# A decoder trunk: each layer opens with its input's norm, and two projections run through it by thirds

## The chip, the cores and the metric

One NeuronCore of one Trainium2 chip. The metric is the device time of one execution in microseconds. The kernel before took 3741.0 us, the median of three executions (3737.36 to 3747.48).

## The reference

Two layers over 1056 tokens of width 1024: a prompt of 1024 tokens, and eight samples of 4 tokens each with a cache of 2048 past tokens. All in float32. What matters here:

```python
h = layer_norm(x, ln0_g, ln0_b)
for l in range(2):
    u = h @ w_in[l]                      # 23 column tiles of 128: z, xbc, dt, q, k, v, qi, ki, wi, glu
    mix = concat(ssd(...), sparse_attention(...), conformer_conv(...)) @ w_out[l]
    h = layer_norm(ALPHA * h + mix, ln1_g[l], ln1_b[l])
    f = gated_causal_conv_ffn(h)         # w_up, width-3 convolution, silu gate, w_down
    h = layer_norm(ALPHA * h + f, ln2_g[l], ln2_b[l])
# returned: h, and the new keys, values, index keys, states and convolution histories of both layers
```

The sparse attention first scores all keys with small index vectors (qi, ki, wi); the samples' index keys lie in pages of 128 tokens in memory, which a page table names.

## The kernel before, in words

Activations lie with the 1024 channels on the partitions, as 8 tiles (KT) of 128 x 1056. A loop of the device (Fori, two rounds) holds one layer. The five engines' programs are written by hand and meet in semaphores. A layer has six stages; each ends in a barrier in which every engine drains and waits for the other three (Stages.end, L459 to 462; the lines L461 and L466 of the trace are its waits and those of the loop's barrier). At the loop's head a second barrier (between_layers, L464) lets SyncE clear all semaphores of a layer.

The norms ln0 (of the input, ahead of the loop), ln1 and ln2 work on three column groups of 352 tokens, the thirds. For ln0 and ln2, TensorE takes the mean of a third's total with one matmul against a matrix of 1/1024 (ln_mean, L781). VectorE subtracts it from the 8 tiles (L1667), ScalarE squares them into four buffers in turn (L1329), and TensorE adds the squares up, one matmul for each tile (ln_var, L797), which also frees the buffers. ScalarE takes the root (L1334), VectorE the reciprocal (L1672) and eight multiplies (L1677), ScalarE applies gain and bias and writes the result to X (L1344). A float32 matmul shows as two records in the trace. ln_all sets the order: VectorE subtracts in all three thirds and then does reciprocal and multiplies third by third; ScalarE squares all three thirds, and then does root and outputs third by third. ln0 works in place on X, ln2 on MIX. ln2 stands at the end of the loop's body, and the stage's barrier behind it.

At the start SyncE loads the input by thirds, then gains, constants and page table. In the loop it asks for the layer's vector VEC, the two convolution histories SSDH and CCH (these lie in tiles 6 and 7 of MIX), and then for a list of loads (LOADS) into a ring of 4 slots: three w_in tiles, six of the eight groups of index pages ("kidx", 16 pages to a group; each page is a register load and a DMA issue of its own, L422 and L423), then the other w_in tiles, and so on. A slot is loaded again when its user is done: the group in slot 0 waits for the product of the first w_in tile, the next two for those of the second and third. Groups 1 and 2 go to a buffer of their own; ScalarE issues them, 16 pages before the first product's copy and 16 between the second's and the third's (load_index_pages, called in ScalarE's loop over N_IDX).

The first stage's jobs (JOBS) are, in order: the first w_in tile (T_KI: index key, dt, wi), the second (T_QI), dup and rotdup (two small products with T_KI's copy), turn (its transposes), the third w_in tile, and two rotations. Jobs take two sets of three PSUM banks in turn; a set is free when ScalarE or VectorE has read it. After T_KI's copy, ScalarE and VectorE pass a softplus to and fro (L1757 to L1769, L1421, L1423); turn waits for its end. The second stage scores the index keys and turns the pages (L890).

When a layer is done, SyncE stores the first two thirds of X to yT, in both layers; the last third goes out behind the loop.

```python
            for t in range(THIRDS):
                ln_mean("ln0", t)
            for t in range(THIRDS):
                ln_var("ln0", t)
            pe.wait_ge(const_loaded, 48)
            with pe.Fori(0, DEPTH) as layer:
                between_layers(pe)
```

Of the kernel before, what the change touches and what calls it, by code (L numbers as in the profile page):

```python
# [182 lines left out]
def build(nc, xT, w_in, w_out, w_up, w_down, vec, ln0, const, pages, cache_k, cache_v, cache_kidx,  # L183
          ssm_in, ssd_in, cc_in, ffn_in, yT, kT_out, v_out, ki_out, ssm_p, ssm_s, ssd_out, cc_out, ffn_out):
    ctx = ExitStack()
    with ctx:
# [178 lines left out]
        def cache_page(name):  # L365
# [21 lines left out]
                                              "scaled", "out")}  # L387
        idx_full, idx_relu, idx_added = sem("index_products"), sem("index_relu"), sem("index_added")
# [133 lines left out]
        def ln_src(name, k, t):  # L522
            return third_of((MIX if name == "ln2" else X)[:, k, :], t)

        def ln_total(name, t):
            return {"ln0": third_of(WORK[:, 0:TOK], t), "ln1": TOTAL[:, t, :], "ln2": third_of(GATE[:, 0:TOK], t)}[name]
# [12 lines left out]
        def _(sp):  # L539

            for t in range(THIRDS):
                sp.dma_start(third_of(X[:, :, :], t), third_of(xT, t)).then_inc(x_loaded[t], 16)
# [4 lines left out]
            with sp.Fori(0, DEPTH) as layer:  # L547
# [78 lines left out]
        def _(pool):  # L626
# [8 lines left out]
            with pool.Fori(0, DEPTH) as layer:  # L635
# [91 lines left out]
                stage.end()  # L727
# [3 lines left out]
        def _(pe):  # L731
# [43 lines left out]
            def ln_mean(name, t):  # L775

                q = LN_FIRST[name] + t
                pe.wait_ge(tot["sum"], q + 1)
                if name == "ln1" and t:
                    pe.wait_ge(tot["centred"], KT * q)  # L780
                pe.matmul(mean_bank(name, t), MEAN[D_MODEL][:, :], ln_total(name, t), start=True, stop=True  # L781
                          ).then_inc(tot["mean"], 1)
# [9 lines left out]
            def ln_var(name, t):  # L792

                q = LN_FIRST[name] + t
                for k in range(KT):
                    pe.wait_ge(tot["squared"], KT * q + k + 1)
                    pe.matmul(var_bank(name, t), MEAN[D_MODEL][:, :], FOUR_SQUARES[:, k % 4, :], start=k == 0, stop=k == KT - 1  # L797
                              ).then_inc(tot["taken"] if k < KT - 1 else tot["var"], 1)
# [23 lines left out]
            for t in range(THIRDS):  # L822
                ln_mean("ln0", t)
# [1668 lines left out]
```

## Time and profile before

| | before |
|---|---|
| median of three executions | 3741.0 us |
| the profiled execution's own time | 3736.99 us |
| its span | 3735.2 us |
| busy share of TensorE, VectorE, ScalarE, GpSimd | 89%, 51%, 33%, 18% |
| chain of waits, share by engine | TensorE 66%, VectorE 15%, ScalarE 7%, SyncE's queue 6%, issue 3%, DMA 2% |
| granted TensorE clock, mean | 0.925 of full speed |

The span is the time from the first to the last instruction on the chip. Busy shares are means over the whole of it. The chain of waits is followed back from the last instruction, at each step to what released it; "issue" in it is time in which the engine waited for nothing that the profile shows. In the list of waits and in timelines, "idle" stands in square brackets, with what ended it behind an arrow. PE is TensorE, DVE VectorE, ACT ScalarE, POOL GpSimd, SP SyncE; a q behind it (SPq, ACTq) is that engine's instruction queue, where DMAs are issued.

### The profile page before, as it was taken

What the parts mean: (1) busy time and instruction counts of PE and PEld (TensorE: products, weight loads), DVE (VectorE), ACT (ScalarE), POOL (GpSimd) and SP (SyncE); (2) the same over time, 40 slices, a digit from 0 to 9 for tenths busy, and PEclk for the clock granted to TensorE, in tenths of its full rate; (3) what the DMA queues carried; (4) which work ended last, traced back from release to release, by engine and by line L of the source; (5) the groups of instructions that cost most, each with busy time, mean ns of one, the idle gap of its engine ahead of it and who ended that gap; (6) DMA issues with size and microseconds to landing.
All of it is one profiled execution on the core that took longest, in us unless ns stands there. A gap on an engine that the chain in (4) does not pass through costs nothing.

```text
span 3735.2 us, 51972 instructions
## 1 busy us (share of the span) xinstructions
PE 3315.5 (89%) x19418; PEld 2675.2 (72%) x19418; DVE 1898.2 (51%) x3006; ACT 1220.3 (33%) x2261; POOL 661.6 (18%) x661
## 2 busy tenths in 40 slices
PE   4899987877989999999868999887779999999995
PEld 2445465644889999999834544665459899999994
DVE  4569774331665434434435797633236644334335
ACT  3246713333342212212222656142343312212213
POOL 0000000011024333333100000000110333333321
PEclk8999998857999999999979999996689999999998
DMA  3111004305201111111021110242150111111111
GB/s 102 41 41 34 29 26 125 94 28 148 72 23 39 47 51 35 51 52 35 28 81 44 34 34 23 70 117 70 57 168 7 37 49 36 53 49 35 54 36 58
DMA packets 169896, 206.62 MB, mean 55 GB/s; under 512 B 61025, under 2 KB 138146, under 8 KB 168738
## 3 DMA queue, kind: packets, MB, share of 16 engines
q1 hardware_dynamic: 143138, 185.36, 16.5%
q10 hardware_dynamic: 26496, 17.84, 1.7%
q8 instruction: 156, 2.56, 0.3%
q14 instruction: 106, 0.87, 0.1%
HBM read 187.17 MB, written 15.96 MB: 54 GB/s over the span
## 4 chain that ended last, share of the span: by engine, by line
PE 66%; DVE 15%; ACT 7%; SPq 6%; issue 3%; DMA 2%; POOL 0%; ACTq 0%; DVEq 0%; POOLq 0%
PE PS L758 42%; PE PS L739 8%; DVE MIX L1708 4%; DVE WORK L1708 2%; SPq L432 2%; SPq L433 2%; PE PS L771 2%; ACT X L1344 2%; PE PS L843 2%; DVE WORK L1896 2%; PE PS L951 1%; ACT WORK L1469 1%; DMA RING<-cache_k 1%; PE PS L797 1%; DVE WORK L1672 1%
## 5 line engine op out<-in xcount | busy, mean ns | idle before, releaser
L758 PE MATMUL PS<-WORK_parts,WHIGH_parts 128*128 128x352 f32 x4224 | 869.5, 328 | 35.2 <-POOL WORK_parts L725 17.7
L758 PEld LDWEIGHTS PS<-WORK_parts,WHIGH_parts 128*128 128x128 f32 x4224 | 723.7, 191 | 38.9 <-issue 20.6
L739 PE MATMUL PS<-X,RING 128*128 128x512 f32 (+1 forms) x2016 | 670.5, 495 | 86.2 <-DMA RING<-w_in 65.8
L758 PE MATMUL PS<-WORK_parts,RING_parts 128*128 128x352 f32 x3168 | 690.8, 326 | 0.0
L739 PEld LDWEIGHTS PS<-X,RING 128*128 128x128 f32 x2016 | 337.9, 194 | 420.1 <-issue 351.0
L758 PEld LDWEIGHTS PS<-WORK_parts,RING_parts 128*128 128x128 f32 x3168 | 545.2, 190 | 0.0
L1708 DVE SCALAR_TENSOR_TENSOR WORK<-WORK,VEC 128x1072 f32<-128x1072 f32 (+1 forms) x236 | 477.3, 2022 | 8.4
L1293 ACT ACTIVATE WORK<-PS 128x32 f32<-128x32 f32 (+11 forms) x412 | 191.0, 514 | 825.1 <-PE PS L758 580.4
L497 POOL TENSOR_TENSOR RING_parts<-RING,WHIGH_parts 128x1024 fp32r<-128x1024 f32 (+2 forms) x184 | 372.1, 2022 | 461.4 <-ACT WHIGH_parts L1293 461.1
L758 PE MATMUL PS<-X_parts,WHIGH_parts 128*128 128x352 f32 x2016 | 435.0, 324 | 0.0
L758 PEld LDWEIGHTS PS<-X_parts,WHIGH_parts 128*128 128x128 f32 x2016 | 345.1, 189 | 0.0
L1706 DVE TENSOR_SCALAR WORK<-WORK,VEC 128x1072 f32<-128x1072 f32 (+1 forms) x90 | 70.6, 784 | 530.1 <-ACT WORK L1293 530.1
L1469 ACT ACTIVATE WORK<-WORK 128x512 bf16<-128x512 f32 x310 | 285.7, 923 | 164.1 <-DVE WORK L1943 164.0
L1293 ACT ACTIVATE WHIGH_parts<-RING 128x1024 fp32r<-128x1024 f32 (+2 forms) x188 | 155.5, 827 | 436.3 <-PE PS L758 418.0
L2316 DVE TENSOR_TENSOR MIX<-MIX,PS 128x1056 f32<-128x1056 f32 x80 | 100.3, 1254 | 286.5 <-PE PS L758 286.5
L771 PE MATMUL PS<-WORK_parts 128*128 128x352 f32 x576 | 144.6, 331 | 0.0
L1708 DVE SCALAR_TENSOR_TENSOR MIX<-WORK,VEC,MIX 128x1296 f32<-128x1296 f32 (+1 forms) x96 | 142.5, 1484 | 3.4
L725 POOL TENSOR_TENSOR WORK_parts<-WORK,WORK_parts 128x1056 fp32r<-128x1056 f32 x44 | 108.2, 2460 | 168.3 <-ACT WORK_parts L1293 168.3
L1293 ACT ACTIVATE WORK_parts<-WORK 128x1056 fp32r<-128x1056 f32 (+1 forms) x56 | 59.4, 1078 | 218.7 <-DVE WORK L2304 218.7
L951 PE MATMUL PS<-CONST,RING 128*128 128x128 f32 x512 | 82.4, 304 | 48.2 <-DMA RING<-cache_k 29.1
L2108 DVE CUSTOM_DVE_ANT_0 WORK<-PS,WORK 128x384 f32<-128x384 f32 (+5 forms) x48 | 41.7, 887 | 152.0 <-PE PS L1101 152.0
L1896 DVE TENSOR_SCALAR_CACHE_REDUCE WORK<-WORK 128x544 bf16<-128x544 f32 (+6 forms) x164 | 116.0, 743 | 0.3
(323 smaller groups left out, 3738.3 us busy)
## 6 DMA issues: line engine op xcount, KB each, us to landing
RING<-w_up SPq DMA_DIRECT2D x88, 512.0 KB, 3.6
RING<-cache_k SPq DMA_DIRECT2D x200, 128.0 KB, 2.2
RING<-cache_v SPq DMA_DIRECT2D x192, 128.0 KB, 2.1
RING<-w_in SPq DMA_DIRECT2D x46, 512.0 KB, 3.7
RING<-w_down SPq DMA_DIRECT2D x80, 256.0 KB, 2.7
RING<-cache_v ACTq DMA_DIRECT2D x64, 128.0 KB, 2.4
RING<-cache_k ACTq DMA_DIRECT2D x56, 128.0 KB, 2.6
yT<-X SPq DMA_DIRECT2D x5, 1408.0 KB, 5.5
```

Source lines behind the costliest of these rows:

```text
L432: page = eng.value_load(PT[0:1, at_page:at_page + 1], min_val=0, max_val=cache_k.shape[0] - 1)
L497: eng.tensor_tensor(low, raw, WHIGH[:, m % 2, 0:w].bitcast(F32), ALU.subtract).then_inc(done, 1)
L725: pool.tensor_tensor(HIDL[:, b, :], HID[:, b, :], HIDH[:, b, :].bitcast(F32), ALU.subtract).then_inc(hid_low, 1)
L739: mm = pe.matmul(job_psum(n, w, first=first), stationary(k), moving(k)[:, first:first + w], start=k == 0, stop=k == k_tiles - 1)
L758: mm = pe.matmul(thirds(n)[:, third, :], a, x[:, third * THIRD:(third + 1) * THIRD], start=k == 0 and part == 0, stop=k == tiles - 1 and p ...
L771: mm = pe.matmul(dst, a[:, w], third_of(x, t), start=k == 0 and part == 0, stop=k == KT - 1 and part == 2)
L951: mm = pe.transpose(key_bank(k)[:, (j % 2 * 2 + t) * P:(j % 2 * 2 + t + 1) * P], cache_page(name)[:, j, t * P:(t + 1) * P], c("ident"))
L1293: return act.activation(dst, src, ACT.Copy)
L1469: ins = act.activation(SCAN_ASIDE[s][:, 0:w], SEL[:, SEL_AT[i]:SEL_AT[i] + w], ACT.Sign, bias=SCAN_TRIED[:, s:s + 1], scale=SCAN_SCALE, ac ...
L1708: ins = dve.scalar_tensor_tensor(out=acc, in0=src[:, k:k + w], scalar=v(col + k), in1=acc, op0=ALU.mult, op1=ALU.add)
L1896: marks.append(step.mark(dve.tensor_scalar(ASIDE[len(marks) % 2][:, 0:x.shape[-1]], x, limit, None, op, ALU.add, accum_out=to)))
L2316: dve.tensor_tensor(y, y, thirds(n), ALU.add).then_inc(free[n % 2], 1)
```

## The change

ln0's place in the loop is the head of its body: in both rounds it norms what lies in MIX, which is the input in the first round and the first layer's sum in the second. ln2 stands behind the loop, once. Gains and biases come from LN0; in the fifth stage GpSimd copies ln2's into it. The sixth barrier of a layer is gone. The new norm has semaphores of its own (opening).

ln_all has a new order: VectorE subtracts in third t+1 before the reciprocal and the multiplies of third t; ScalarE squares third t+1 between the root and the outputs of third t. TensorE takes three means, two variances, then the first two w_in tiles' products of third 0 (open_third), the variance of third 2, and the products of thirds 1 and 2. SyncE asks for the three w_in tiles first; VEC comes ahead of page group 0; then SyncE issues page group 1 as well and waits for the norm's last output before it loads the histories. ScalarE issues 8 pages of group 2 behind the norm and 8 at the job dup. yT is stored once, by thirds, behind the loop.

```diff
 def ln_src(name, k, t):
-    return third_of((MIX if name == "ln2" else X)[:, k, :], t)
+    return third_of((X if name == "ln1" else MIX)[:, k, :], t)
...
 # SyncE
-    sp.dma_start(third_of(X[:, :, :], t), third_of(xT, t)).then_inc(x_loaded[t], 16)
+    sp.dma_start(third_of(MIX[:, :, :], t), third_of(xT, t)).then_inc(x_loaded[t], 16)
...
-    sp.dma_start(VEC[:, :], vec[layer, :, :]).then_inc(vec_loaded, 16)
-    sp.dma_start(SSDH[:, :, :], ssd_in[layer, :, :, :]).then_inc(hist_loaded, 16)
-    sp.dma_start(CCH[:, :, :], cc_in[layer, :, :, :]).then_inc(hist_loaded, 16)
     for n, name in enumerate(LOADS):
         kind, slot = name[0], n % NSLOT
+        if name == ("kidx", 0):
+            sp.dma_start(VEC[:, :], vec[layer, :, :]).then_inc(vec_loaded, 16)
+        elif n == NSLOT:
+            load_index_pages(sp, layer, KEPT_APART[0], 0, 16)
+            sp.wait_ge(opening["out"], KT * THIRDS)
+            sp.dma_start(SSDH[:, :, :], ssd_in[layer, :, :, :]).then_inc(hist_loaded, 16)
+            sp.dma_start(CCH[:, :, :], cc_in[layer, :, :, :]).then_inc(hist_loaded, 16)
...
-    for t in range(THIRDS - 1):
-        sp.wait_ge(tot["out"], KT * (LN_FIRST["ln2"] + t + 1))
-        store(third_of(yT, t), third_of(X[:, :, :], t))
-    sp.wait_ge(stored, 16 * 12)
-    sp.wait_ge(stage_done, 4 * 6)
-store(third_of(yT, THIRDS - 1), third_of(X[:, :, :], THIRDS - 1))
+    sp.wait_ge(stored, 16 * 10)
+for t in range(THIRDS):
+    sp.wait_ge(tot["out"], KT * (LN_FIRST["ln2"] + t + 1))
+    store(third_of(yT, t), third_of(X[:, :, :], t))
...
 # GpSimd, fifth stage
+    pool.tensor_copy(LN0[:, :], VEC[:, V_LN2G:V_LN2G + 2 * KT])
...
 # TensorE: the means and variances of ln0 ahead of the loop are gone; in the loop
-    for n in range(N_IDX):
+    def open_third(t):
+        for n in range(2):
+            w = weights(JOBS[n])
+            for k in range(KT):
+                pe.wait_ge(opening["out"], KT * t + k + 1)
+                mm = pe.matmul(thirds(n)[:, t, :], w[:, k, :], third_of(X[:, k, :], t),
+                               start=k == 0, stop=k == KT - 1)
+            if t == THIRDS - 1:
+                mm.then_inc(full[n % 2], 1)
+
+    for t in range(THIRDS):
+        ln_mean("ln0", t)
+    ln_var("ln0", 0)
+    ln_var("ln0", 1)
+    open_third(0)
+    ln_var("ln0", 2)
+    open_third(1)
+    open_third(2)
+    for n in range(2, N_IDX):
         project(n)
     stage.end()
...
 # ScalarE
 def ln_all(name, gcol, bcol, params):
-    for t in range(THIRDS):
-        ln_squares(name, t, range(KT))
+    ln_squares(name, 0, range(KT))
     for t in range(THIRDS):
         ln_rstd(name, t)
+        if t + 1 < THIRDS:
+            ln_squares(name, t + 1, range(KT))
         ln_out_parts(name, t, range(KT), gcol, bcol, params)
...
-ln_all("ln0", 0, KT, LN0)
 with act.Fori(0, DEPTH) as layer:
     between_layers(act)
+    ln_all("ln0", 0, KT, LN0)
+    load_index_pages(act, layer, KEPT_APART[1], 0, 8)
     act.wait_ge(vec_loaded, 16)
     act.activation(EXPA[:, :], VEC[:, V_ALOG:V_ALOG + SSD_HEADS], ACT.Exp)
...
     for n in range(N_IDX):
-        if n in (0, 2):
-            load_index_pages(act, layer, KEPT_APART[n // 2], 0, 16)
+        if n == 2:
+            load_index_pages(act, layer, KEPT_APART[1], 8, 8)
         project(n)
...
-    ln_all("ln2", V_LN2G, V_LN2B, VEC)
-    stage.end()
+ln_all("ln2", V_LN2G, V_LN2B, VEC)
...
 # VectorE
 def ln_all(name):
+    for k in range(KT):
+        ln_centre(name, 0, k)
     for t in range(THIRDS):
-        for k in range(KT):
-            ln_centre(name, t, k)
-    for t in range(THIRDS):
+        if t + 1 < THIRDS:
+            for k in range(KT):
+                ln_centre(name, t + 1, k)
         ln_inverse(name, t)
         for k in range(KT):
             ln_scale(name, t, k)
```

## Rows read from the trace of the kernel before

**Rows 1.** Chain of waits, start and boundary of the layers: start, length in us, what.

```profile
8.57 10.55 DMA PT<-pages
...
1857.75 12.07 PE PS L797 x40
...
1896.36 4.21 issue
...
1903.54 3.96 DMA RING<-w_in
```

**Rows 2.** Timeline, first projections of layer 0: start, us, engine, line, operation, [idle before].

```profile
66.10 17.43 ACTq L423 DMA_DIRECT2D WHIGH<-cache_kidx  x16
...
68.39 33.60 PE L739 MATMUL PS<-X,RING 128*128 128x512 f32 x96 [30.44 <-DMA RING<-w_in]
...
86.50 1.05 ACT L1293 ACTIVATE WORK<-PS 128x1056 f32<-128x1056 f32 x1 [21.19 <-PE PS L739]
...
92.86 1.08 ACT L1423 ACTIVATE MIX<-MIX 8x1056 f32<-8x1056 f32 x1 [0.75 <-DVE MIX L1763]
...
95.26 1.25 DVE L1769 TENSOR_TENSOR WORK<-WORK,MIX 8x1056 f32<-8x1056 f32 x1
...
101.91 5.97 PE L739 MATMUL PS<-WORK,CONST 64*128 64x512 f32 x12
...
109.79 16.08 PE L739 MATMUL PS<-X,RING 128*128 128x512 f32 x48
```

**Rows 3.** Timeline, the norm ahead of layer 0 and the first barrier.

```profile
19.15 10.44 DVE L1667 TENSOR_TENSOR X<-X,PS 128x352 f32<-128x352 f32 x24
...
38.07 2.35 DVE L1672 RECIPROCAL WORK<-WORK 128x352 f32<-128x352 f32 x1 [8.49 <-ACT WORK L1334]
...
41.02 4.68 ACT L1344 ACTIVATE X<-X,LN 128x352 f32<-128x352 f32 x8 [2.98 <-DVE X L1677]
...
62.46 1.28 ACT L1376 ACT_TABLE_LOAD   x1 [0.56 <-SPq L553]
```

**Rows 4.** Timeline, end of layer 0 and start of layer 1.

```profile
1855.13 1.40 DVE L2325 TENSOR_TENSOR WORK<-WORK,MIX 128x352 f32<-128x352 f32 x3
...
1857.16 13.24 ACT L1329 ACTIVATE WORK<-MIX 128x352 f32<-128x352 f32 x24 [8.87 <-DVE MIX L1667]
...
1948.94 16.39 PE L739 MATMUL PS<-X,RING 128*128 128x512 f32 x48
```

**Rows 5.** Timeline of SyncE's queue in layer 0: the page loads.

```profile
66.89 77.98 SPq L423 DMA_DIRECT2D RING<-cache_kidx  x64
...
146.51 37.41 SPq L423 DMA_DIRECT2D RING<-cache_kidx  x32
```

**Rows 6.** SyncE's waits, 60 to 250 us: us in total, times, longest.

```profile
SPq L422 <- PE PS L739: 3.2, 2, 1.9
```

**Rows 7.** Timeline of TensorE, end of the index stage in layer 1.

```profile
2025.28 0.44 PE L890 MATMUL PS<-CONST,RING 128*128 128x128 f32 x2 [1.52 <-DMA RING<-cache_kidx]
```

**Rows 8.** Windows: us, then busy us of each engine (instructions), granted clock, DMA.

```profile
25.00:36.00 11.00, 11.00 (x37) 6.95 (x37) 4.59 (x11) 8.76 (x18) 0.00 (x0) 1.00 0.00 1
68.00:73.00 5.00, 4.61 (x6) 2.02 (x7) 0.00 (x0) 0.00 (x0) 0.00 (x0) 0.50 0.77 244
1975.00:1985.00 10.00, 9.91 (x28) 4.30 (x28) 6.43 (x23) 2.92 (x4) 1.48 (x1) 0.52 0.13 28
```

**Rows 9.** ScalarE's groups by line: roots and their table loads (busy us, mean ns).

```profile
L1334 ACT ACTIVATE WORK<-PS,EPSC 128x352 f32<-128x352 f32 x15 | 8.2, 546 | 7.9 <-PE PS L789 7.8
...
L1334 ACT ACT_TABLE_LOAD x5 | 6.4, 1283 | 0.1
```

**Rows 10.** Timeline, the last norm and the stores of y.

```profile
3689.46 10.44 DVE L1667 TENSOR_TENSOR MIX<-MIX,PS 128x352 f32<-128x352 f32 x24
...
3712.80 17.02 SPq L560 DMA_DIRECT2D yT<-X  x3
...
3724.29 4.68 ACT L1344 ACTIVATE X<-MIX,VEC 128x352 f32<-128x352 f32 x8 [2.98 <-DVE MIX L1677]
```

More of the change, by code:

```diff
@@ L387, in build @@
                                               "scaled", "out")}
+        opening = {n: sem("opening_" + n) for n in ("mean", "centred", "squared", "taken", "var", "rstd", "inverse",
+                                                    "scaled", "out")}
         idx_full, idx_relu, idx_added = sem("index_products"), sem("index_relu"), sem("index_added")
@@ L522, in ln_src, with ln_sems @@
         def ln_src(name, k, t):
-            return third_of((MIX if name == "ln2" else X)[:, k, :], t)
+            return third_of((X if name == "ln1" else MIX)[:, k, :], t)
+        def ln_sems(name):
+            return opening if name == "ln0" else tot
         def ln_total(name, t):
-            return {"ln0": third_of(WORK[:, 0:TOK], t), "ln1": TOTAL[:, t, :], "ln2": third_of(GATE[:, 0:TOK], t)}[name]
+            return TOTAL[:, t, :] if name == "ln1" else third_of(GATE[:, 0:TOK], t)
         def mean_bank(name, t):
@@ L1281, in _ @@
                                       lambda k: pe.wait_ge(hid_low, first + k + 1))
-                for t in range(THIRDS):
-                    ln_mean("ln2", t)
-                for t in range(THIRDS):
-                    ln_var("ln2", t)
-                stage.end()
+            for t in range(THIRDS):
+                ln_mean("ln2", t)
+            for t in range(THIRDS):
+                ln_var("ln2", t)
         @block.scalar
@@ L1344, in ln_out_parts @@
                     act.activation(third_of(X[:, k, :], t), src, ACT.Identity, bias=bias, scale=scale
-                                   ).then_inc(tot["out"], 1)
+                                   ).then_inc(sems["out"], 1)
             def ln_all(name, gcol, bcol, params):
-                for t in range(THIRDS):
-                    ln_squares(name, t, range(KT))
+                ln_squares(name, 0, range(KT))
                 for t in range(THIRDS):
                     ln_rstd(name, t)
+                    if t + 1 < THIRDS:
+                        ln_squares(name, t + 1, range(KT))
                     ln_out_parts(name, t, range(KT), gcol, bcol, params)
@@ L1415, in project @@
                                else KTL[:, j - T_K, :] if j < T_Q else QT[:, j - T_Q, :])
-                        copy(dst, job_psum(n)).then_inc(f, 1)
+                        if n < 2:
+                            copy(in_thirds(dst), thirds(n)).then_inc(f, 1)
+                        else:
+                            copy(dst, job_psum(n)).then_inc(f, 1)
                     if j == T_KI:
@@ L1662, in ln_centre @@
             def ln_centre(name, t, k):
[L1663 removed]
+                q, sems = LN_FIRST[name] + t, ln_sems(name)
                 if k == 0:
[L1665 removed]
+                    dve.wait_ge(sems["mean"], q + 1)
                 s = ln_src(name, k, t)
[L1667 removed]
+                dve.tensor_tensor(s, s, mean_bank(name, t), ALU.subtract).then_inc(sems["centred"], 1)
             def ln_inverse(name, t):
[L1670 to L1673 removed]
+                q, sems = LN_FIRST[name] + t, ln_sems(name)
+                dve.wait_ge(sems["rstd"], q + 1)
+                dve.reciprocal(RSTD[:, t, :], RSTD[:, t, :]).then_inc(sems["inverse"], 1)
+                dve.wait_ge(sems["inverse"], q + 1)
             def ln_scale(name, t, k):
                 s = ln_src(name, k, t)
[L1677 removed]
+                dve.tensor_tensor(s, s, RSTD[:, t, :], ALU.mult).then_inc(ln_sems(name)["scaled"], 1)
             def ln_all(name):
+                for k in range(KT):
+                    ln_centre(name, 0, k)
                 for t in range(THIRDS):
[L1682 to L1684 removed]
+                    if t + 1 < THIRDS:
+                        for k in range(KT):
+                            ln_centre(name, t + 1, k)
                     ln_inverse(name, t)
@@ L2325, in _ @@
                                     dve.tensor_tensor(total, total, ln_src("ln2", j, t), ALU.add).then_inc(tot["sum"], 1)
-                ln_all("ln2")
-                stage.end()
+            ln_all("ln2")
 def _constants():
```

45 lines of the change are left out of this document (17 added, 28 removed).

## The prediction

> **What bounds the kernel now.** I read the page's busy shares first: TensorE is busy 89% of the span and heads the chain of waits, so what the change can win lies in stretches where TensorE stands still. Next the chain, at the three places where a norm stands alone: the start, the boundary between the layers and the end. At the start the chain runs through the load of the page table, which lands at 8.57 + 10.55 = 19.12 us, then through the norm, then through the first weights (the boundary shows 3.96 us of waiting for w_in) [rows 1]; the timeline shows TensorE's first projection at 68.39 us, after 30.44 us idle [rows 2]. At the boundary there is also a stretch of 4.21 us in which nothing runs, directly after the stage's end and before the loop's first instruction [rows 1]: the return to the loop's head.
>
> Last I followed the norm and the first projections in the timelines. In the norm every engine works in blocks of three thirds: all 24 subtractions (10.44 us), all squares (13.24 us at the boundary), then, third by third, a reciprocal of 2.35 us and eight multiplies, with eight outputs behind them [rows 3, 4]. TensorE has little to do in it, and afterwards two projections in a row (33.60 us for two) while ScalarE and VectorE wait [rows 2]. Behind that, SyncE's queue is nearly the bound up to the end of the index stage: it issues 32 page loads in 37.41 us (18.7 us for a group of 16), waits for TensorE only 3.2 us in the first 190 us of the layer, and TensorE waits 1.52 us for its last pages [rows 5 to 7]. Whatever moves the third w_in projection's end moves the rest with it, since the next SyncE group is issued at just that point and every stage ends in a barrier. I call this end T, counted from the release of the loop's barrier, B.
>
> **Before, per layer.** Layer 0: B would lie at 19.12 + 0.56 = 19.7 us (0.56 us is what the barrier took [rows 3]); the third projection ends at 109.79 + 16.08 = 125.9 [rows 2], that is T = 106.2. Layer 1: the totals of ln2 are ready at 1855.13 + 1.40 = 1856.5 [rows 4]. With the changed order the loop's return comes first: 4.2 + 0.1 + 0.6 us of barrier give B = 1861.4. The third projection ends at 1948.94 + 16.39 = 1965.3 [rows 4], T = 103.9.
>
> **After, step by step, in us after B.** A 352-column matmul takes 12.07/40 x 2 = 0.60 us at the full clock [rows 1], 1.2 at half. TensorE comes out of an idle stretch, so its granted clock is taken as half for 5 us, as at 68 to 73 us [rows 8].
> - Three means 3.6; variance of third 0: one matmul at half, seven at full: 9.0. VectorE subtracts third 0 from 1.2 and third 1 behind it, out of the way.
> - ScalarE squares until 8.4, loads the table of the root (1.28, as now) and takes it (0.55 [rows 9]): 10.2. Squares of third 1 (13.24/24 = 0.55 each [rows 4], behind matmuls of 0.60): 15.0. The reciprocal (2.35) ends at 12.6 beside it. Outputs of third 0 (4.68 [rows 3]): 19.7.
> - TensorE follows the outputs: first projection of this third 20.3, second 25.0. Only then comes its variance of third 2, and the last four squares wait for that through four buffers: squares end at 27.9, variance 29.8.
> - Outputs of third 1: 32.7; root 33.2, reciprocal 35.6; the outputs begin 41.02 - 40.42 = 0.6 behind it [rows 3]: 36.1 to 40.8. This is the norm's end.
> - TensorE has no gap from 25.0 on: third 1 of both projections 29.8 + 9.4 = 39.2, third 2 of the first 43.9, of the second 48.6.
> - ScalarE must now issue 8 page loads before it copies the first product: half of 17.43 = 8.7 [rows 2], then a table load (1.28 [rows 9]) and an exponential of eight columns (some 0.2): copy at 51.2. Before, all 16 issues lay beside the first projection and cost nothing; now that cover is gone, and the copy is 7.3 late against the product at 43.9. This is the wait that is added.
> - The softplus chain between ScalarE and VectorE is short of cover too. From the copy's start to ScalarE's next free moment 92.86 + 1.08 - 86.50 = 7.4, to VectorE's end 95.26 + 1.25 - 86.50 = 10.0 [rows 2]. So the second product is copied at 58.6 to 59.7, rotdup (half of 5.97 [rows 2]) runs 59.7 to 62.7, VectorE is free at 61.2 for the one multiply that the next step needs, and from rotdup's end to the third projection's start it takes 109.79 - 101.91 - 2.98 = 4.9 less rotdup's 2.98, or 1.9: 64.7. With its 16.1 us [rows 2]: T = 80.8 at the full clock.
> - SyncE: the vector, three w_in and two histories took 66.89 - 62.46 = 4.4 [rows 3, 5]. With two groups of pages (one is new here, 16 issues moved over from ScalarE) that is 41.8 at the latest; the histories in it now wait for the norm's end at 40.8, and then comes the group that waits for the first product at 43.9. With the next one: 44.1 + 37.4 = 81.5. So T can't count for less than 81.5.
> - TensorE has idle gaps of 3.7 and 4.4 us around dup. After such gaps the clock may be down; rotdup at half is 3 us more, the start of the third projection 2.5 more. I take 1.0 on top of 81.5: T = 82.5.
>
> Gains: 106.2 - 82.5 = 23.7 in layer 0, 103.9 - 82.5 = 21.4 in layer 1. w_in's wait and the norm's tail are in them; the index stage behind T is as before, since its groups are issued from T on.
>
> **The last norm.** The subtractions start at 3689.46 and the outputs end at 3724.29 + 4.68 = 3728.97 [rows 10]: 39.5 us. In the new order, at the full clock and without projections in between: root of third 0 at 6.8, squares of third 1 11.2, outputs 15.9, root 16.5, squares 20.8, outputs 25.5, root 26.1, reciprocal 28.5, outputs 29.1 to 33.8. Gain 5.7. The last store's way home stays. Leaving the loop costs nothing that I can see: SyncE's last store is issued by 3712.80 + 17.02 = 3729.82, under 0.9 us behind the last output though the loop's end lies between [rows 10]. Bounds: nothing, or 4.2 as on the way back [rows 1]; I take nothing, the nearer row.
>
> **Costed at nothing.** The 0.2 us copy of the gains on GpSimd stands where that engine waits for TensorE; if it did not, it is 0.2 a layer. The two layer-0 stores of y that go away were issued while the norm ran. The input's other buffer changes no duration.
>
> New is that roots and squares alternate on ScalarE. In this trace 15 roots have 5 table loads between them [rows 9], one for each of five norms, though ln1 alternates the same way: I count no load more. The Trainium skill ("ScalarE: Activation LUTs", "Table sets: the hidden batching unit") asks to batch by table set, since a change of set costs a load; by that rule, were the square outside the root's set, each of the three norms would have four loads more, about 15 us in all. The trace speaks against it.
>
> **Sum.** 23.7 + 21.4 + 5.7 = 50.8 us off the profiled execution's 3736.99 us: 3686.2. The median shown is 4.0 us above that execution (3741.0), which gives 3690. I say 3688. Bounds of the terms: with the full clock from B on, T = 79 (SyncE moves along); with a half clock for 10 us, as at 1975 to 1985 us [rows 8], and again at rotdup, T = 88.5; the end 4 to 6.5. That is 37 to 59 us: the likeliest case's own range is 3678 to 3704.
>
> **Rivals.**
> 1. *The queues of page loads set the pace.* SyncE has a group more, and ScalarE's 8 issues stand before the copy. If the norm runs some 6 us longer and page issue is a little slower than 18.7 us a group, T is 92: gains 14.2 + 11.9 + 5.7, so 3705. For it: SyncE is near its limit already [rows 6]. Against: its first two groups lie beside the norm.
> 2. *The thirds don't overlap.* If each third in effect waits for the whole norm, only w_in's wait (some 6.5 us a layer) is won, and the uncovered page issues and table (10 us a layer) eat that and the end's gain: about 3738, no change. Against: no wait in the diff ties the first third to the last.
> 3. *TensorE stays at half clock in the opening*, the mechanism on the other side. Fed in pieces behind ScalarE it would take 1.2 us per matmul: first product 80, second 89, the third projection's start 104.5, T = 123. That is 17 and 19 us worse, less 5.7: 3767. It decides against the change from T = 108 on. Against: in the norm at 25 to 36 the same kind of feeding has a granted clock of 1.00 [rows 8]. The Trainium skill ("TensorE: Matmul & The Clock Gate", "HAM oscillation") warns of just such work in short bursts; the trace agrees only after idle stretches, not while matmuls follow each other.
>
> **How the numbers follow.** Forecast 0.72, rival 1 0.18, rival 2 0.05, rival 3 0.05. The first two are faster by more than 0.3% (11 us, about what a measurement of this kernel tells from no change): 0.90 faster, 0.05 same, 0.05 slower. The range takes in the forecast's bounds and most of rival 1: 3674 to 3712.
>
> **What would show it.** Right: w_in lands while VectorE subtracts; the first projections' matmuls begin near B + 15 and the second one ends near B + 49; ScalarE issues 8 page loads between its last output and the copy; the third projection ends near 102 us and 1944 us; the last output comes some 34 us after the last norm's first subtraction. Wrong: a granted clock of 0.5 through the thirds, the third projection later than B + 92, table loads between squares and roots, or an index stage that has grown longer from T to its end.

## The result, and the profile after

| | before | after |
|---|---|---|
| median of the runs | 3739.4 us (3737.4 to 3747.5, 4 runs) | 3682.6 us (3681.0 to 3688.1, 4 runs) |
| profiled execution / its span | 3736.99 / 3735.2 us | 3682.55 / 3680.7 us |
| TensorE busy / mean granted clock | 89% / 0.93 | 90% / 0.93 |

The changed kernel is faster by 1.6%: ratio 0.9842 [0.983, 0.9854]. The forecast was 3688 (3674 to 3712). The changed kernel run again on another chip gave 3685.9 us, ratio 0.9843 [0.983, 0.9855].

Where the time went is read from marks that both traces have: the first TensorE instruction behind the barriers, the last totals of ln2, the last output.

| stretch | before, us | after, us | gain | forecast |
|---|---|---|---|---|
| start to index stage, layer 0 | 135.62 | 110.89 | 24.7 | 23.7 |
| index stage, layer 0 | 69.32 | 67.23 | 2.1 | 0 |
| from there to the totals of ln2 | 1651.59 | 1654.38 | -2.8 | 0 |
| totals to index stage, layer 1 | 118.56 | 91.27 | 27.3 | 21.4 |
| from there to the last totals | 1714.29 | 1717.76 | -3.5 | 0 |
| last norm, totals to last output | 39.59 | 33.31 | 6.3 | 5.7 |
| last output to the end of the span | 6.23 | 5.86 | 0.4 | 0 |

The sum is 54.5 us of span, against 50.8 forecast. The three stretches with a forecast gave 58.3; the four that were put at nothing took 3.8 back between them. A second trace of the changed kernel (again, below) puts two of these elsewhere: 1650.8 us where the table has 1654.4, and 1724.4 where it has 1717.8.

The opening of layer 0 in the changed kernel, TensorE's timeline (start, us, engine, line, operation, count, [idle before and who ended it]); it answers to the 30.44 us of idle and the 33.60 us of projections in [rows 2]:

```profile
19.97 3.88 PE L789 MATMUL PS<-WORK,MEAN 128*128 128x352 f32 x6 [19.97 <-SPq L558]
23.64 5.74 PE L805 MATMUL PS<-WORK,MEAN 128*128 128x352 f32 x16
30.42 5.00 PE L805 MATMUL PS<-WORK,MEAN 128*128 128x352 f32 x16 [1.03 <-ACT WORK L1353]
35.26 9.63 PE L879 MATMUL PS<-X,RING 128*128 128x352 f32 x32
44.72 4.90 PE L805 MATMUL PS<-WORK,MEAN 128*128 128x352 f32 x16
49.45 19.10 PE L879 MATMUL PS<-X,RING 128*128 128x352 f32 x64
70.89 2.10 PE L746 MATMUL PS<-WORK,CONST 64*128 64x512 f32 x6 [2.34 <-ACT WORK L1317]
78.36 4.01 PE L746 MATMUL PS<-WORK,CONST 64*128 64x512 f32 x6 [5.38 <-ACT WORK L1317]
...
84.28 16.85 PE L746 MATMUL PS<-X,RING 128*128 128x512 f32 x48
```

The reader is to see the third's two projections (L879) between the variances (L805), a TensorE that has hardly a gap from 30 to 68.5 us, and then two gaps of 2.34 and 5.38 us that ScalarE ends. ScalarE beside it, from the last squares on:

```profile
45.57 2.27 ACT L1353 ACTIVATE WORK<-MIX 128x352 f32<-128x352 f32 x4 [5.37 <-PE PS L805]
...
55.83 4.68 ACT L1368 ACTIVATE X<-MIX,LN 128x352 f32<-128x352 f32 x8 [2.98 <-DVE MIX L1705]
59.87 8.40 ACTq L425 DMA_DIRECT2D WHIGH<-cache_kidx  x8
68.30 1.28 ACT L1402 ACT_TABLE_LOAD   x1 [7.79 <-issue]
...
69.71 1.03 ACT L1317 ACTIVATE WORK<-PS 128x1056 f32<-128x1056 f32 x1
```

The eight page issues stand between the norm's last output and the copy of the first product (69.71), as the prediction had it. SyncE's queue, the same stretch:

```profile
20.30 1.43 SPq L614 DMA_DIRECT2D RING<-w_in  x3
...
42.60 18.39 SPq L425 DMA_DIRECT2D WHIGH<-cache_kidx  x16
...
64.66 56.01 SPq L425 DMA_DIRECT2D RING<-cache_kidx  x48
...
122.32 37.43 SPq L425 DMA_DIRECT2D RING<-cache_kidx  x32
```

w_in is asked for while VectorE subtracts. From the first product (64.66) to 159.75 us SyncE issues 80 pages with one small store between them. TensorE waits 1.34 us for the last of them, and 17.05 us later stage 3 begins:

```profile
161.07 0.44 PE L914 MATMUL PS<-CONST,RING 128*128 128x128 f32 x2 [1.34 <-DMA RING<-cache_kidx]
...
178.12 1.12 PE L746 MATMUL PS<-X,RING 128*128 128x512 f32 x2 [0.91 <-DVEq L463]
```

The windows of the opening (us; busy us of PE, PEld, DVE, ACT, POOL; then the granted clock, DMA share, GB/s), against [rows 8]: no half clock while the projections by thirds follow each other, 0.64 in the stretch with the two gaps. The 1.00 of the first window doesn't fit its first matmuls: the three means took 3.88 us there (first row of TensorE's timeline), 3.59 us in layer 1, where the clock from 1834.66 to 1838.20 reads 0.55, and 2.04 us in the last norm. So TensorE did begin at about half pace in both layers, as the prediction took it.

```profile
20.00:36.00 16.00, 14.97 (x41) 9.12 (x42) 12.94 (x26) 12.64 (x24) 0.00 (x0) 1.00 0.41 130
36.00:50.00 14.00, 14.00 (x49) 8.97 (x48) 9.25 (x17) 8.35 (x17) 0.00 (x0) 1.00 0.13 30
50.00:69.00 19.00, 18.55 (x63) 11.59 (x61) 5.92 (x9) 8.23 (x15) 0.00 (x0) 1.00 0.22 52
69.00:84.00 15.00, 7.73 (x20) 4.55 (x21) 9.27 (x9) 6.22 (x7) 0.00 (x0) 0.64 0.20 43
```

The boundary in the chain of waits (start, length, what), against the 4.21 us in [rows 1]. L1725 is the line of VectorE's loop, its row the branch back; L468 is the first instruction of the next round:

```profile
1831.21 0.07 DVEq L1725
...
1832.49 1.56 issue
1834.05 0.09 DVEq L468
```

Layer 1's third projection and the last norm, in the timeline, against [rows 4, 10]:

```profile
1897.58 16.44 PE L746 MATMUL PS<-X,RING 128*128 128x512 f32 x48
...
3641.61 6.98 DVE L1695 TENSOR_TENSOR MIX<-MIX,PS 128x352 f32<-128x352 f32 x16
...
3670.16 4.68 ACT L1368 ACTIVATE X<-MIX,VEC 128x352 f32<-128x352 f32 x8 [2.98 <-DVE MIX L1705]
```

### The profile page after: what moved, and what is told of

It reads as the page before. It is cut to its first block, busy times and chain, and to the rows that moved or that the text cites. A ratio compares the mean times of both kernels' runs of the same rounds, so it can differ in the third digit from the quotient of the medians.

```text
span 3680.7 us, 51974 instructions
## 1 busy us (share of the span) xinstructions
PE 3313.3 (90%) x19418; PEld 2684.5 (73%) x19418; DVE 1897.1 (52%) x3006; ACT 1217.8 (33%) x2262; POOL 661.8 (18%) x663
## 3 DMA queue, kind: packets, MB, share of 16 engines
q8 instruction: 156, 2.56, 0.3%
## 4 chain that ended last, share of the span: by engine, by line
PE 66%; DVE 15%; SPq 6%; ACT 6%; issue 3%; DMA 2%; POOL 0%; ACTq 0%; DVEq 0%; POOLq 0%; PEldq 0%
PE PS L765 42%; PE PS L746 6%; DVE MIX L1738 4%; DVE WORK L1738 2%; PE PS L778 2%; SPq L434 2%; PE PS L847 2%; SPq L435 2%; DVE WORK L1926 2%; SPq L425 1%; SPq L424 1%; ACT X L1368 1%; ACT WORK L1498 1%; PE PS L975 1%; DMA RING<-cache_k 1%
## 5 line engine op out<-in xcount | busy, mean ns | idle before, releaser
L746 PE MATMUL PS<-X,RING 128*128 128x512 f32 (+1 forms) x1824 | 603.7, 493 | 20.5 <-ACT MIX L1438 8.1
L746 PEld LDWEIGHTS PS<-X,RING 128*128 128x128 f32 x1824 | 304.6, 193 | 319.9 <-issue 317.7
L975 PE MATMUL PS<-CONST,RING 128*128 128x128 f32 x512 | 82.3, 303 | 49.0 <-DMA RING<-cache_k 30.2
```

Of the source, the lines that this page charges most:

```text
L746: mm = pe.matmul(job_psum(n, w, first=first), stationary(k), moving(k)[:, first:first + w], start=k == 0, stop=k == k_tiles - 1)
L975: mm = pe.transpose(key_bank(k)[:, (j % 2 * 2 + t) * P:(j % 2 * 2 + t + 1) * P], cache_page(name)[:, j, t * P:(t + 1) * P], c("ident"))
```

## The experiments

Ten kernels were run, each beside runs of the kernel before on the same chip; "again" is the changed kernel unedited. Ratios are against the kernel before on the same chip. again, old_order, whole and pages_later ran on one chip, half_group, both_gaps, tile_order and end_barrier on a second, whole_late_w_in and before_again on a third; the kernel before took 3745.9, 3745.7 and 3743.9 us there. Where two kernels of different chips are compared in us, these are medians of different chips.

### again: the changed kernel, unedited

> The changed kernel once more, unedited, on the chip and beside the kernel before that the next three runs are held against. It also gives a second trace. Theory (the gain is what the openings and the last norm show: 26.8 us at the start of layer 0's third stage, 51.2 at layer 1's, 54.5 at the end): 3682 us, and the same positions within 1 us at both openings. In the first trace 2.8 us of layer 0's gain and 3.6 of layer 1's were given back between the attention stage and the next totals. If that belongs to the change, it is there again, at the same place; if it is TensorE's clock, which stood at 0.95 instead of 1.00 of full speed in one stretch of that trace, it moves or vanishes.

Measured: 3685.9 us, ratio 0.9843 [0.983, 0.9855]. The openings repeat: the index stage begins at 110.97, stage 3 at 178.17 (110.89 and 178.12 in the first trace); in layer 1 the index stage begins 89.2 us behind TensorE's first mean, 89.1 in the first trace. In stretches that the change doesn't touch the two traces differ by 3.6 us (stage 3 of layer 0 to the totals) and 6.7 us (index stage of layer 1 to the last totals). The 2.8 us that layer 0 gave back in the first trace are gone here (0.8 us gained instead), so a difference of that size behind the opening is not shown to be the change's.

### old_order: the norm in its old order

```diff
-ln_var("ln0", 0); ln_var("ln0", 1); open_third(0); ln_var("ln0", 2); open_third(1); open_third(2)
+for t in range(THIRDS): ln_var("ln0", t)
+for t in range(THIRDS): open_third(t)
 # ScalarE: all squares first; VectorE: all subtractions first
```

> The changed kernel with the norm's old order alone: VectorE subtracts and ScalarE squares all three thirds before the first reciprocal, and TensorE's third variance stands ahead of the first projections. Theory (the new order is worth little in the opening, since TensorE works without a gap from the first outputs on, and more at the end): the norm's last output 4 to 5 us later in each opening, the copy of the first product with it, and 6.3 us at the last norm: 16 us slower than the changed kernel, 3698. Rival (the order carries the gain, as the thirds can't follow one another without it): the openings go back by the better part of their 25 us, 3725 or more.

Measured: 3705.4 us, ratio 0.9894 [0.9879, 0.9909], 19.5 us above again (the theory had 16). TensorE's six third-projections then stand in one block, and SyncE's group behind the first product starts at 69.65 instead of 64.66:

```profile
42.03 31.51 PE L879 MATMUL PS<-X,RING 128*128 128x352 f32 x96 [3.89 <-ACT X L1366]
```

```profile
69.65 56.00 SPq L425 DMA_DIRECT2D RING<-cache_kidx  x48
```

The norm's end moves by only 1.5 us and the third projection's end by 1.7, but stage 3 of layer 0 begins 8.3 us later (186.43), and in layer 1, counted from B, 8.7. What counts is SyncE's 5 us, and a longer end of the index stage (below). The old order also costs the last norm 7.6 us (41.06 against 33.42 in again).

### whole: the first two projections whole behind the norm

```diff
-ln_var("ln0", 0); ln_var("ln0", 1); open_third(0); ln_var("ln0", 2); open_third(1); open_third(2)
-for n in range(2, N_IDX): project(n)
+for t in range(THIRDS): ln_var("ln0", t)
+pe.wait_ge(opening["out"], KT * THIRDS)
+for n in range(N_IDX): project(n)
 # ScalarE copies the first two products in one piece again
```

> The changed kernel with the first two projections in one piece behind the whole norm, as before; the norm's new order, the early request for w_in and everything else stay. Theory (projecting by thirds is worth about half of an opening's gain, as the two projections take 33.6 us in one piece but only 8 of their 28.7 us in thirds lie behind the norm's last output): the norm ends some 5 us earlier without them, both products together some 20 us later, but the softplus chain and the page loads find cover again: third projection's end 12 us later in each layer, 3707. Rival (the early w_in and the barrier are the gain, and the chain of page loads and softplus eats what the thirds win): within 4 us of the changed kernel, 3682 to 3687.

Measured: 3717.2 us, ratio 0.9927 [0.9912, 0.9941], 31.4 above again (the theory had 25). The projections wait for the norm's end, the third one ends 11.1 us later (112.28), SyncE's group starts at 76.48, stage 3 at 192.60 (+14.4; in layer 1, counted from B, +15.7). The view of SyncE's queue ends at 120 us, so its count is not the whole group:

```profile
56.87 34.29 PE L746 MATMUL PS<-X,RING 128*128 128x512 f32 x96 [10.95 <-ACT X L1365]
```

```profile
76.48 42.81 SPq L425 DMA_DIRECT2D RING<-cache_kidx  x37
```

So half of what the change wins on this chip (3745.9 less 3685.9, 60 us) is the overlap of the thirds with the norm.

### whole_late_w_in: whole, and w_in asked for behind the norm

```diff
+for early in range(T_XBC): sp.dma_start(RING[:, early, ...], w_in[layer, early, ...])  # behind the wait for the norm's end
-sp.dma_start(RING[:, slot, ...], w_in ...)                                              # in front, for these three
```

> The kernel with the first two projections whole behind the norm (whole, 3717.2 us), and w_in asked for late as before the change: SyncE issues the vector and two groups of page loads first, waits for the norm's end, and only then asks for the three w_in. Theory A (what the early request is worth is the time from the norm's end to w_in's landing): in whole the norm ends at 56.9 us, SyncE's queue is free at 61.3, and w_in takes about 4.0 us from there, so the first projection starts at about 65.3 us instead of 56.9. That is 8.4 us a layer; SyncE's next group, which waits for the first product, moves from 76.5 to about 85, so all of it counts: about 3734 us, the third projection's end at 120.7. Theory B (only w_in's own 4.0 us count, because page issue has room to catch up): about 3725 us. Theory C (the early request is worth nothing here, the queue and the softplus chain end later anyway): 3717 us.

Measured: 3727.1 us, ratio 0.9951 [0.9935, 0.9968], 9.9 above whole, on another chip; the two intervals just meet, so the rows count for more. Stage 3 begins 6.6 us later in layer 0. In layer 1, counted from B, the index stage begins 3.4 us later and stage 3 1.6. The mechanism is theory A's, the price lies between A and B: SyncE, without three requests in front, is through its pages 2 us earlier (59.34, not 61.3), the projections start 6.2 us later than in whole and the next group 5.2 (SyncE's view ends at 130 us):

```profile
59.34 1.37 SPq L575 DMA_DIRECT2D RING<-w_in  x3
...
81.70 48.24 SPq L425 DMA_DIRECT2D RING<-cache_kidx  x40
```

```profile
63.05 33.33 PE L750 MATMUL PS<-X,RING 128*128 128x512 f32 x96 [17.43 <-DMA RING<-w_in]
```

So the early request is worth some 8 to 10 us by itself. With w_in asked for at this place, behind the norm's end, the thirds could not run in the changed kernel's order at all: the variance of the last third, which the norm's end needs, stands behind the first third's projections, which need w_in. By that the early request is also a condition of the other 31 us; this is argued from the order of the waits, and no run shows it.

### pages_later: ScalarE's eight page issues behind the softplus

```diff
-load_index_pages(act, layer, KEPT_APART[1], 0, 8)          # ahead of the copy
-    load_index_pages(act, layer, KEPT_APART[1], 8, 8)
+    load_index_pages(act, layer, KEPT_APART[1], 0, 16)     # behind T_QI's copy
```

> The changed kernel with ScalarE's 8 page issues between its last output and the first product's copy moved behind the second product's copy, to the other 8. Theory (SyncE's queue ends at the same time as this chain: its three groups from the first product on are issued without a pause, 64.66 to 120.67 us, and the third projection ends just inside): the third projection ends 5.4 us earlier in each layer, TensorE waits that much longer for the last pages at the end of the index stage, and the time stays: 3680 to 3683. Rival (the 8 issues are the path, as the chain of waits has them): 5.4 us a layer, 3671.5.

Measured: 3694.6 us, ratio 0.9867 [0.985, 0.9884], 8.7 above again (the two intervals just meet); neither theory had that. The third projection does come 6.2 us earlier (the index stage begins at 104.74). But SyncE's queue is where it was, so TensorE runs ahead of the pages, waits 8.36 us for the last (again: 1.29), and what follows goes at a lower granted clock: 0.50 from 160 to 165 us and 0.90 from 165 to 170 (again: 1.00 from 155 to 170):

```profile
161.99 0.69 PE L914 MATMUL PS<-CONST,RING 128*128 128x128 f32 x2 [8.36 <-DMA RING<-cache_kidx]
...
181.75 18.79 PE L746 MATMUL PS<-X,RING 128*128 128x512 f32 x55 [0.91 <-DVEq L463]
```

```profile
160.00:165.00 5.00, 3.01 (x12) 1.77 (x12) 0.42 (x1) 0.00 (x0) 0.00 (x0) 0.50 0.71 214
```

Stage 3 begins 3.6 us later than in again, and in layer 1, counted from B, 2.2. The rest of the 8.7 lies in stretches that drift between traces of one kernel too. A step made earlier made the kernel no faster.

### half_group: eight pages of group 4 moved from SyncE to ScalarE

```diff
-load_index_pages(sp, layer, name[1], 0, 16)
+load_index_pages(sp, layer, name[1], 0, 8 if name[1] == 4 else 16)
+    load_index_pages(act, layer, 4, 8, 8)                  # ScalarE, behind T_QI's copy
```

> The changed kernel, with 8 of the 16 page issues of the group that waits for the second product (group 4) taken from SyncE and given to ScalarE, behind its other 8. Theory (SyncE's queue is the path from the first product on, but only just: its third group starts 0.9 us after the third projection's end in layer 0 and 1.6 us after it in layer 1): the group starts with the projection's end, the wait for the last pages falls from 1.3 and 1.8 us to under 1, and the time is 2 to 3 us less than the changed kernel's, at the edge of what can be told. Rival (ScalarE's 8 issues before the copy are the path): no change.

Measured: 3689.7 us, ratio 0.9858 [0.9842, 0.9875]: no gain, where the theory had 2 to 3 us. SyncE's 40 pages take 55.15 us, where 40 without a wait would take 46.7 (56.01/48 each): it waits 8.6 us for the third projection, and then 2.1 us between its store and the next group (0.85 in the changed kernel), for a buffer whose pages TensorE must first have turned. With T where it was, a shorter queue has nothing to start on.

```profile
63.96 55.15 SPq L425 DMA_DIRECT2D RING<-cache_kidx  x40
119.30 0.61 SPq L565 DMA_DIRECT2D ki_out<-WORK  x1
122.04 37.57 SPq L425 DMA_DIRECT2D RING<-cache_kidx  x32
```

### both_gaps: both at once

half_group, and ScalarE's pages out of the way: five between the fourth and fifth square of the last third, where it waits 5.37 us anyway, two behind the last root, nine behind T_QI's copy.

> As half_group, and ScalarE's 8 page issues ahead of the first product's copy gone: 5 stand in its idle gap between the first and the last four squares of third 2, 2 behind the last root, 9 behind the second product's copy. Theory (after the change two chains end together, ScalarE's page loads with the softplus, and SyncE's queue; only both together shorten the opening): the third projection ends 6 us earlier in each layer, SyncE's next group with it, the wait for the last pages stays under 1.5 us, so TensorE's clock doesn't fall there: 7 us a layer, 14 less than the changed kernel. Rival (moving the issues does harm by itself, since with it alone the kernel was 9 us slower): no faster than the changed kernel.

Measured: 3676.5 us, ratio 0.9822 [0.9807, 0.9837], 9.4 below again (14 expected); the two intervals just meet, so the rows are the better witness. Stage 3 begins at 170.38 (-7.8), and SyncE's later group at 114.50. In layer 1, counted from B, stage 3 begins 4.9 us earlier: there TensorE waits 2.28 us for the last pages, and 19.69 us pass from there to stage 3 instead of 16.87:

```profile
64.03 48.82 SPq L425 DMA_DIRECT2D RING<-cache_kidx  x40
...
114.50 37.52 SPq L425 DMA_DIRECT2D RING<-cache_kidx  x32
```

So the opening has two chains that end together, ScalarE's issues and softplus up to T, and SyncE's queue from the first product on. Either alone gives nothing (pages_later put ScalarE's pages elsewhere than this kernel, but the third projection ended as early, 94.98 against 93.84); both together do.

### tile_order: a better order on TensorE

```diff
-open_third(0); ln_var("ln0", 2); open_third(1); open_third(2)         # both projections of a third
+open_third(0, 0); ln_var("ln0", 2)                                    # third, projection
+for t, n in ((1, 0), (0, 1), (2, 0), (1, 1), (2, 1)): open_third(t, n)
 # ScalarE's pages: 2 behind the last root, 2 behind the last output, 12 + 8 behind T_QI's copy
```

> As both_gaps, but TensorE takes the thirds in another order: third 0 of the first product, the variance of third 2, then third 1 of the first product, third 0 of the second, third 2 of the first, and the second's other two. ScalarE issues 2 pages behind the last root, 2 behind the last output and 12 with group 4's 8 behind the second product's copy. Theory (SyncE's groups start with the first product, which this order has 4 to 5 us earlier; the softplus runs beside the second product): the first product full near 59.4 us in layer 0, the third projection's end near 93, some 9 us a layer, 18 less than the changed kernel. Rival (TensorE works without a gap in the thirds, so the order of its matmuls changes nothing): as both_gaps within 2 us.

Measured: **3668.7 us**, ratio 0.98 [0.9782, 0.9819], 17 below again: the lowest median of this study, and below both that were given. Its interval meets that of both_gaps, so what the order adds to both_gaps is read from the rows. The last third's variance no longer waits behind a projection that nobody needs yet, and the first product is full earlier:

```profile
34.37 4.90 PE L878 MATMUL PS<-X,RING 128*128 128x352 f32 x16
39.10 4.90 PE L805 MATMUL PS<-WORK,MEAN 128*128 128x352 f32 x16
43.84 23.83 PE L878 MATMUL PS<-X,RING 128*128 128x352 f32 x80
...
73.11 15.68 PE L746 MATMUL PS<-X,RING 128*128 128x512 f32 x48 [0.31 <-DVE WORK L1807]
```

```profile
61.71 0.33 SPq L575 DMA_DIRECT2D MIX<-cc_in  x1
62.91 46.63 SPq L425 DMA_DIRECT2D RING<-cache_kidx  x40
...
111.19 37.42 SPq L425 DMA_DIRECT2D RING<-cache_kidx  x32
```

The third projection ends at 88.79 instead of 101.13 (both_gaps: 93.84). SyncE now goes from its histories straight into the next group (62.04 to 62.91) and issues its 40 pages at the pace of an unhindered queue: in this kernel its queue is what is left. So of the 5 us that TensorE's order wins over both_gaps, stage 3 of layer 0 sees 2.0 (168.40): TensorE waits 2.38 us for the last pages, with a longer way to stage 3 behind it. In layer 1 stage 3 begins 5.2 us earlier than in both_gaps, counted from B, 2.7 of them in the stretch behind this wait, which is only 0.85 there.

### end_barrier and before_again: the loop's return

```diff
 pool.wait_ge(ffn_saved, 2 * FF)
+stage.end()          # and the same at the loop's end on TensorE, ScalarE and VectorE
```

> The changed kernel with a stage's barrier of the four engines put back at the end of the loop's body, ahead of the return. Theory (the return to the loop's head took 4.21 us in the kernel before because there all engines left a barrier and returned at the same moment, with a cold start for each; in the changed kernel three of them have long been there when VectorE arrives, and it takes 1.56): the stretch in which nothing runs is near 4.2 us again. Rival (the length hangs on where the loop's code lies): near 1.6 us as in the changed kernel.

> The kernel before, unedited, with a second trace. If the return to the loop's head costs about 4 us whenever all engines leave the last stage's barrier together, its chain shows again 3.7 to 4.3 us of nothing between that barrier and the loop's first instruction (4.21 in the first trace, 3.73 in end_barrier, 1.55 to 1.74 in the kernels without that barrier). If that stretch varies by chance from trace to trace, it shows some other value, down to 1.6. The stage starts should lie within 3 us of the first trace's: 135.6, 204.9, 750.7, 1975.1, 2042.3, 2589.5.

Measured: end_barrier 3695.6 us (one run), the kernel before 3747.3 (one run). The stretch in which nothing runs, in the chain of each, end_barrier first (L1728 is the branch of VectorE's loop there):

```profile
1833.77 0.07 DVEq L1728
1833.84 3.73 issue
```

```profile
1896.38 4.23 issue
```

Where all engines leave a barrier right before the loop's end, this stretch took 4.21, 4.23 and 3.73 us; in the nine traces without that barrier 1.55 to 1.74. But the two don't begin at the same point. In end_barrier VectorE's branch ends at 1833.84 and the stretch begins there. In the changed kernel the branch ends at 1831.28, under VectorE's last additions, which end at 1832.49; the 1.56 us are what is left of the return behind them. From the branch to the next round's first instruction it is 2.77 us there (2.77 to 2.96 in the nine) against 3.73 to 4.23. So the theory holds for the stretch, and that it varies by chance does not; but some 1.2 us of the difference is cover, and only 0.8 to 1.5 a longer return. ScalarE and GpSimd, which return some 7 us before VectorE in the changed kernel, also took about 2.7 us there, against some 3.6 to 4.2 with the barrier. TensorE's branch was not longer with it: 3.5 to 4.1 us in the nine traces, 3.4 to 3.5 in the three.

As a whole a barrier costs more than this: from the totals to the index stage of layer 1 end_barrier takes 94.6 us, the changed kernel 91.3 and 91.4; from the last totals to the last output 36.8 against 33.3 and 33.4. That is 6.6 us for two barriers; the other 3 of its 9.7 above again, one run against several on another chip, are not shown to be the barriers'. In before_again the stage starts lie within 0.3 us of the first trace's up to 1975.1; the last two come 2.6 and 3.1 us later, where 3 were allowed for.

## Why the prediction was right, step by step

**The opening.** In us after B, both layers. Layer 0 is counted from the forecast's B, 19.7 (the barrier was released at 19.9, which takes 0.2 off each), layer 1 from 1834.6:

| step | forecast | layer 0 | layer 1 |
|---|---|---|---|
| root of third 0 | 10.2 | 10.3 | 9.0 |
| both projections of third 0 | 25.0 | 25.2 | 23.9 |
| last squares | 27.9 | 28.1 | 26.8 |
| norm's end | 40.8 | 40.8 | 39.5 |
| second projection's end | 48.6 | 48.9 | 47.6 |
| copy of the first product | 51.2 | 50.0 | 48.4 |
| copy for T_QI | 58.6 | 57.5 | 55.9 |
| third projection's end | 82.5 | 81.4 | 79.4 |

Layer 1 leads from the first root on, by 1.3 us: TensorE's matmuls at half pace took less time there (means and first variance 8.3 us, 9.4 in layer 0). The added wait is there and was 1 us too dear: 8.40 us of issues against 8.7, and the first of them begins before the last output's end. SyncE's bound of 81.5 came as 82.3 in layer 0 (64.66 and 32 pages of 56.01/48 us each): the prediction was right that T can't count for less than this queue. pages_later and half_group show that the two bounds lie that close.

**The failed size.** The largest error is a term of B in layer 1: the loop's return was carried over at 4.2 us [rows 1] into a kernel without the barrier in front of it; there 1.56 us of it stood uncovered. That is 2.7 us of the 5.9 by which layer 1's opening beat its forecast; the rest is T, 79.4 for 82.5.

**What was called unchanged.** That the index stage behind T stays as it was held for its chain and was off by 2.1 us in layer 0. Before, TensorE waited 2.78 us for the last pages there and stage 3 began 19.58 us later; after, 1.34 and 17.05 (rows above). The prediction had read this wait in layer 1 alone, where it was 1.52 [rows 7]. Layer 0 of the kernel before:

```profile
185.36 0.44 PE L890 MATMUL PS<-CONST,RING 128*128 128x128 f32 x2 [2.78 <-DMA RING<-cache_kidx]
```

The stretches behind gave back 2.8 and 3.5 us; the second trace of the same kernel differs from the first by 3.6 and 6.7 in these stretches, so this isn't put down to the change. The openings and the last norm alone won 58.3 us for 50.8; that the whole came to 54.5, nearer the forecast, is owed to these stretches and not to the terms of the sum.

**The last norm** gave 6.3 for 5.7: the last root ends 25.6 us behind the first subtraction instead of 26.1, and the outputs follow it. **Table loads** stayed at five for 15 roots, as [rows 9]; after:

```profile
L1358 ACT ACTIVATE WORK<-PS,EPSC 128x352 f32<-128x352 f32 x15 | 8.2, 546 | 9.4 <-PE PS L797 7.8 <-PE PS L805 1.5
L1358 ACT ACT_TABLE_LOAD x5 | 6.4, 1283 | 0.1
```

The prediction's "no load more" was off by one all the same: the load at the first square, once before, now comes in both rounds (19.97 and 1834.66). It takes 1.28 us while TensorE is at its means, and squares wait for VectorE behind it, so it cost nothing.

**The rivals.** Rival 1 (the queues set the pace) is true as a mechanism and cost nothing near T = 92, since nothing made the norm longer; old_order shows its price when the first product is 5 us late. Rival 2 (no overlap) is the kernel whole: 3717, not 3738. Rival 3 (half clock) did not come: 1.00 in the windows from 36 to 69 us, and in layer 1 from 1848 to 1882; the half pace ended with the means and the first matmuls behind them.

**Parts, by the runs:** of the 60 us won on the first experiments' chip, 31 are lost when the thirds don't overlap the norm (whole). The norm's old order alone loses 19.5, 7.6 of them in its trace at the last norm, which whole keeps in the new order; so the two losses overlap only in part and don't add up. w_in in front is worth 8 to 10 more, measured without the overlap. What remains, 16.9 us by whole_late_w_in against the kernel before on its chip, was not taken apart: in it lie the last norm's order, some 6 us, the removed barrier, some 3 by end_barrier, and the norm's order in the opening.

## What to carry to other kernels

When two chains end together, shortening one was worth nothing here, and cost something when the engine that then waited came back at a lower clock; find the second chain in the queues' rows before moving anything. A transfer that is asked for early can be worth more by the order that it makes possible than by its own wait; here that is argued from the waits. A projection that follows a norm can begin with the first third, but then each engine's order should put what others wait for (the last variance, the first product) ahead of what only fills time.

## What the runs showed of the hardware

**The loop's return was longer for VectorE where all engines made it at once.** From VectorE's branch to the first instruction of the next round, 2.77 to 2.96 us in nine traces where the engines reach the loop's end apart, and 3.73, 4.21 and 4.23 in three where all leave a barrier right in front of it. In the nine, 1.2 us of it lie under VectorE's last operation. The Trainium skill ("Runtime: NRT & Kernel Launch", "Instruction fetch mechanics") says that a taken branch breaks the sequential prefetch of code and can stall until its target is fetched. A gap at the return agrees with it; that VectorE's is longer when the engines return together, and TensorE's is not, is what the runs add; why was not measured.

**A short wait costs more than itself.** In all twelve traces the end of the index stage was read in both layers: TensorE's wait for the last pages, and the time from there to stage 3, which is the same work each time. Ten waits of 0.85 to 1.90 us were followed by 16.9 to 17.1 us at a granted clock of 0.90, fourteen of 2.28 to 9.42 us by 18.1 to 20.5 at 0.71 to 0.82. The kernel before shows both, 1.52 us in layer 1 and 2.78 in layer 0:

| kernel before | wait, us | from its end to stage 3, us | TensorE busy in it, us | granted clock in it |
|---|---|---|---|---|
| layer 1, 2025.28 to 2042.31 | 1.52 | 17.03 | 13.99 | 0.90 |
| layer 0, 185.36 to 204.94 | 2.78 | 19.58 | 16.55 | 0.74 |

The same 75 matmul records keep TensorE busy 2.56 us longer, and the rest of the stretch is 3.0 us in both, as it is in all 24. So 1 to 3 us come on top of a wait that is itself under 3 us.

**Runs of one kernel differ behind equal openings.** In the two traces of the kernel before the stage starts agree within 0.3 us up to 1975 us; from the index stage of layer 1 to the last totals one takes 1714.3 and the other 1724.3, and the spans are 3735.2 and 3745.5. Marks behind the stretch in question tell what a change did; the end of the span alone would not have told 3 us from nothing.
